# Softmax sums applied to outputs instead of probabilities, and modulation rows weighed on GpSimd, in a three-layer transformer kernel

## The reference, cut to what matters

```
shift, scale, gate = split(silu(c) @ ada_w + ada_b, 3)
h = rmsnorm(x, g) * (1 + scale) + shift
x = x + gate * mixer(h)
```

## Time and profile before

| | |
|---|---|
| median of 3 runs | 1159.05 us (1158.66 to 1159.08) |
| the profiled execution's own time | 1159.5 us |
| its span in the trace | 1157.7 us |
| busy in the span: PE, DVE, ACT, POOL | 1099.8, 734.3, 649.0, 419.3 us |
| layer 1's attention | about 106 to 398 us |
| layer 2's attention | about 565 to 752 us |

### The profile page before, as it was taken

The page is one execution under the profiler, slowest core; times in us unless marked ns, Lnnn a source line. Parts: engine busy times, 40 slices in busy tenths (PEclk is TensorE's granted clock), DMA queues, the critical chain, the costliest instruction groups (busy, mean ns, idle before and its releaser), DMA issues.

```text
span 1157.7 us, 20235 instructions
## 1 busy us (share of the span) xinstructions
PE 1099.8 (95%) x7430; PEld 900.7 (78%) x7430; DVE 734.3 (63%) x1590; ACT 649.0 (56%) x1355; POOL 419.3 (36%) x513
## 2 busy tenths in 40 slices
PE   5999999999998899999899999999999999999996
PEld 2678778877885689877688887898878777888785
DVE  7575766676568625363787787745767775527745
ACT  5604555555556526643677777846567753457733
POOL 2633012212120334675400002416654326456781
PEclk9999999999999999999999999999999999999998
DMA  9741424322114521130201101053212403213112
GB/s 373 253 163 46 176 107 162 133 108 101 46 29 173 204 81 37 40 109 35 57 14 34 65 10 47 1 166 87 73 46 78 151 19 128 91 56 121 44 37 73
DMA packets 34253, 109.33 MB, mean 94 GB/s; under 512 B 4516, under 2 KB 7076, under 8 KB 33772
## 3 DMA queue, kind: packets, MB, share of 16 engines
q1 hardware_dynamic: 34156, 108.05, 27.7%
HBM read 101.39 MB, written 2.11 MB: 89 GB/s over the span
## 4 chain that ended last, share of the span: by engine, by line
PE 75%; DVE 12%; ACT 5%; issue 3%; POOL 2%; DMA 2%; SPq 1%; DVEq 0%; POOLq 0%; ACTq 0%
PE PS L677 31%; PE PS L660 15%; PE PS L794 8%; PE PS L782 7%; PE PS L983 6%; PE PS L1051 3%; DMA AF<-wstream 2%; PE PS L712 2%; DVE AD L2372 1%; ACT AF L1272 1%; DVE AF L2069 1%; POOL AR L2553 1%; DVE AR L2273 1%; PE PS L884 1%; PE PS L693 1%
## 5 line engine op out<-in xcount | busy, mean ns | idle before, releaser
L2553 POOL TENSOR_TENSOR AR<-AF,AR 128x256 fp32r<-128x256 f32 x396 | 304.5, 802 | 585.2 <-ACT AR L1152 585.2
L677 PE MATMUL PS<-AR 128*128 128x512 f32 (+1 forms) x2208 | 450.5, 360 | 4.7 <-POOL AR L2553 1.4
L677 PEld LDWEIGHTS PS<-AR 128*128 128x128 f32 x2208 | 364.0, 189 | 72.6 <-issue 10.5
L660 PE MATMUL PS<-AR 128*128 128x256 f32 (+4 forms) x1284 | 244.9, 327 | 6.7 <-ACT AF L1272 1.7
L660 PEld LDWEIGHTS PS<-AR 128*128 128x128 f32 (+1 forms) x1284 | 179.8, 190 | 41.7 <-issue 20.6
L1281 ACT ACTIVATE AF<-PS 128x512 f32<-128x512 f32 (+3 forms) x192 | 124.6, 649 | 100.0 <-PE PS L782 96.0
L1272 ACT ACTIVATE AF<-PS,AF 128x512 f32<-128x512 f32 (+3 forms) x192 | 140.8, 733 | 27.2 <-DVE AF L2349 18.3
L782 PE MATMUL PS<-AF 128*128 128x128 f32 x864 | 127.4, 274 | 8.4 <-DVE AF L1990 5.9
L782 PEld LDWEIGHTS PS<-AF 128*128 128x128 f32 x864 | 100.1, 140 | 32.9 <-issue 15.5
L1152 ACT ACTIVATE AR<-AF 128x1024 fp32r<-128x1024 f32 x99 | 103.3, 1052 | 35.3 <-PE PS L983 27.9
L794 PE MATMUL PS<-AF 128*64 128x128 f32 x1728 | 115.3, 278 | 3.4 <-DVE AF L1997 2.5
(11 more groups left out here) (216 smaller groups left out, 1147.2 us busy)
## 6 DMA issues: line engine op xcount, KB each, us to landing
AF<-wstream SPq DMA_DIRECT2D x171, 512.0 KB, 5.0
AF<-x_in SPq DMA_DIRECT2D x2, 1024.0 KB, 8.5
AD<-rows SPq DMA_DIRECT2D x4, 512.0 KB, 5.9
out<-AF SPq DMA_DIRECT2D x16, 128.0 KB, 1.9
AF<-AF SPq DMA_DIRECT2D x28, 64.0 KB, 2.0
AF<-rpb_band SPq DMA_DIRECT2D x8, 224.0 KB, 5.2
BIAS<-rpb_band SPq DMA_DIRECT2D x8, 224.0 KB, 4.7
AF<-ctx_in SPq DMA_DIRECT2D x1, 1024.0 KB, 5.5
```

Source lines behind the costliest of these rows:

```text
L660: mm = pe.matmul(out, stationary, moving, start=i == 0, stop=i == len(products) - 1)
L677: mm = pe.matmul(out[:, 0:t1 - t0], a, b, start=k == 0 and i == 0, stop=k == nk - 1 and i == 2)
L2553: ins = pool.tensor_tensor(w[:, 1, at:at + 256], raw(c)[:, at:at + 256], w[:, 0, at:at + 256].bitcast(F32), ALU.subtract)
```

## The change

Three things are done.

First, for pairs 0 to 5 of layer 1 and 0 to 6 of layer 2 (`N_LATE`) the probabilities are no longer multiplied by the inverse sum. PE turns them as soon as the exponentials are done. ACT leaves the sums of a whole pair side by side. At the first step of the next pair DVE inverts them (`invert_sums`), SP stores the 128 x 12 or 128 x 8 numbers element by element into DRAM so that tokens lie in a row, waits until they are there, and loads each head's row broadcast over 64 partitions (`spread_sums`). One pair later DVE multiplies the gated output by these rows (`scale_output`).

Second, layer 3's modulation rows are no longer made of 48 matmuls in layer 1. GpSimd multiplies each raw piece in place by the condition's value for each of its rows, and adds the halves and the pieces (`mix_rows`), 24 pieces at the start of layer 2's attention; PE then sums over the partitions with 6 matmuls against ones (`mixed_rows`, filler of step 19), and transposes once, at step 23.

Third, the order of pieces changes: ada2 stands behind B.uq1 and ahead of B.o0, layer 2's modulation (ada1) spreads over layer 1's attention, with ada1.4 and ada1.5 in the last pair.

```diff
-ADA_GROUPS = {0: ((0,), (1,), (2,), (3,), (4, 5)), 1: (tuple(range(6)),), 2: ((0, 1, 2), (3, 4, 5))}
+ADA_GROUPS = {0: ((0,), (1,), (2,), (3,), (4, 5)), 1: (tuple(range(6)),), 2: (tuple(range(6)),)}
+N_LATE = {"A": 6, "B": 7, "C": 0}
...
 def between_a(p):
-    return (None, "ada1.0", "ada1.2", "ada1.4", "ada1.5.t", "ada2.1", None, None)[p]
-def late_a(p):
-    return (None, "ada1.1", "ada1.3", "ada1.5", "ada2.0", None, None, "ada2.2")[p]
+    return (None, "ada1.0", "ada1.1", "ada1.2", None, "ada1.3", None, None)[p]
...
-        return [["ada2.2.t"], ["ada2.3"], ["ada2.4"], ["ada2.5"], ["ada2.5.t"], late[0:1], late[1:3],
+        return [["ada1.4:0"], ["ada1.4:1"], ["ada1.5:0"], ["ada1.5:1"], ["ada1.5.t"], late[0:1], late[1:3],
...
 def fillers_b(p, step):
     if step == 3:
-        return []
+        return {5: ["mix2.sum"], 6: ["ada2.5.t"]}.get(p, [])
...
 def turn(n):
-    pe.wait_ge(p_ready, n + 1)
+    if late(n):
+        pe.wait_ge(exp_done, n + 1)
+    else:
+        pe.wait_ge(p_ready, whole_at[n] + 1)
...
+def mixed_rows():
+    out = acc_open("mix2.sum")
+    pe.wait_ge(mix_step, MIX_STEPS)
+    for b in range(6):
+        g = b % 4
+        mm = pe.matmul(out[32 * g:32 * g + 12, :], ONE_ROW[:, 10 - 2 * b:22 - 2 * b], MIXED[:, b],
+                       start=b < 4, stop=b >= 2)
...
+def scale_output(layer, p):
+    rows = SUM_ROWS[layer]
+    dve.wait_ge(sums_in, 32 * (late_at(layer, p) + 1))
+    ins = dve.tensor_tensor(OG[:, p, :], OG[:, p, :], rows[:, 0:S], ALU.mult)
...
+def mix_rows():
...
+    for b in range(6):
+        for q in range(4):
+            pool.wait_ge(*raw_loaded(c))
+            pool.tensor_tensor(w, w, by, ALU.mult).then_inc(mix_step, 1)
...
+            if summed:
+                add_to(*summed)
...
+            ins = pool.tensor_tensor(total, w[:, 0], w[:, 1], ALU.add)
...
-for first, after in ((2, "B.o1"), (4, "B.o2"), (6, "B.o5")):
+for p, after in ((2, "ada2.2.2"), (3, "ada2.3.2"), (4, "ada2.4.1"), (5, "ada2.5.1"), (6, "B.o0"), (7, "B.o4")):
     if name == after:
-        load_roped_queries(first)
-        load_roped_queries(first + 1)
+        load_roped_queries(p)
+        spread_sums("B", p - 2)
+        if p == N_PAIR - 1:
+            spread_sums("B", p - 1)
...
+def spread_sums(layer, p):
+    if p >= N_LATE[layer]:
+        return
+    n, i = per_pair[layer], late_at(layer, p)
+    sp.wait_ge(sums_ready, i + 1)
+    sp.dma_start(sums_dram[p % 2, 0:2 * n * P].rearrange("(i q) -> q i", q=P),
+                 SUMS_OF[layer][2][:, p % 2].rearrange("p h t -> p (h t)"), allow_slow_non_contiguous=True).then_inc(sums_stored, 16)
+    sp.wait_ge(sums_stored, 16 * (i + 1))
+    if i:
+        sp.wait_ge(scaled, i)
+    for h in range(2):
+        sp.dma_start(SUM_ROWS[layer][ROWS_OF[h], 0:n * P],
+                     sums_dram[p % 2:p % 2 + 1, h * n * P:(h + 1) * n * P].to_broadcast([64, n * P])).then_inc(sums_in, 16)
```

More of the change, by code:

```diff
@@ L68, in chunk_plan @@
         split(f"A.q{p}", f"A.g{p}")
[L69 to L72, removed]
+        name = between_a(p)
+        if name:
+            ada(int(name[3]), int(name[5]))
     split("A.o0")
-    for late in (3, 4, 5):
-        ada(2, late)
+    for late in (4, 5):
+        ada(1, late)
     split(*[f"A.o{j}" for j in range(1, KD)])
@@ L592, in is_c, with late, late_at, late_sums @@
             return n >= 2 * B_END
+        def late(n):
+            return units[n]["pair"] < N_LATE[units[n]["layer"]]
+        whole = [n for n in range(len(units)) if not late(n)]
+        whole_at = {n: i for i, n in enumerate(whole)}
+        def late_at(layer, p):
+            return p + (N_LATE["A"] if layer == "B" else 0)
+        def late_sums(n):
+            u = units[n]
+            t = n // 2 - start_of[u["layer"]] - per_pair[u["layer"]] * u["pair"]
+            sums, sinks = (SUMS_OF[u["layer"]][i][:, u["pair"] % 2] for i in range(2))
+            return sums[:, u["half"], t:t + 1], sinks[:, u["half"], t:t + 1]
         def score_bank(n):
@@ L721, in ada_columns @@
                 out = acc_open(name)
-                rows, i = tasks[f"ada{layer}.{b}"]
+                rows, i = tasks["mix2.sum" if layer == 2 else f"ada{layer}.{b}"]
                 pe.wait_ge(acc_read[rows], i)
@@ L1991, in normalise, with invert_sums, late_work @@
                                   ALU.mult).then_inc(p_ready, 1)
+            def invert_sums(layer, p):
+                dve.wait_ge(exp_done, pair_scored(layer, p))
+                sums, sinks, inverse = (SUMS_OF[layer][i][:, p % 2] for i in range(3))
+                if layer == "A":
+                    step(dve.tensor_tensor(sums, sums, sinks, ALU.add))
+                signal(dve.reciprocal(inverse, sums), sums_ready, late_at(layer, p) + 1)
+            def scale_output(layer, p):
+                rows = SUM_ROWS[layer]
+                dve.wait_ge(sums_in, 32 * (late_at(layer, p) + 1))
+                ins = dve.tensor_tensor(OG[:, p, :], OG[:, p, :], rows[:, 0:S], ALU.mult)
+                if layer == "A":
+                    ins = dve.tensor_tensor(OGC[:, p, :], OGC[:, p, :], rows[:, S:T], ALU.mult)
+                signal(ins, scaled, late_at(layer, p) + 1)
+            def late_work(layer, m):
+                n = per_pair[layer]
+                p, s = (m - start_of[layer]) // n, (m - start_of[layer]) % n
+                if s == 0 and 1 <= p <= N_LATE[layer]:
+                    invert_sums(layer, p - 1)
+                if s == 0 and 2 <= p <= N_LATE[layer] + 1:
+                    scale_output(layer, p - 2)
+                if s == n - 1 and p == N_LATE[layer] == N_PAIR - 1:
+                    scale_output(layer, p - 1)
             def gate_output(m):
@@ L2024, in attend @@
                         negmax(2 * m + 1)
+                    if m < m1 and not late(2 * m):
                         normalise(2 * m)
@@ L2027, in attend @@
                         gate_output(m - 2)
+                    if m < m1 and not late(2 * m):
+                        normalise(2 * m + 1)
                     if m < m1:
-                        normalise(2 * m + 1)
+                        late_work("A" if early else "B", m)
                     if later and m0 < m <= m1:
@@ L2764, in others @@
                     sp.dma_start(ROPE, rope[1]).then_inc(sp_rope, 16)
-                if name == "B.o0":
+                if name == "ada2.1.0":
                     sp.wait_ge(kr_split, 1)
@@ L3032 @@
     out = nc.dram_tensor("out", (P, KD, S), F32, kind="ExternalOutput").ap()
-    build(nc, rows_dram=rows_dram, out=out, **args)
+    sums_dram = nc.dram_tensor("sums", (2, 2 * T), F32, kind="Internal").ap()
+    build(nc, rows_dram=rows_dram, sums_dram=sums_dram, out=out, **args)
     result = run_bass_kernel_spmd(nc, [arrays], core_ids=[0]).results[0]["out"]
```

85 lines of the change are left out of this document (73 added, 12 removed).

## The result

The changed kernel takes 1178.43 us (median of 4 runs, 1177.94 to 1178.96), the kernel before 1159.07 in the same comparison: 1.0165 times as long, 95% interval 1.0148 to 1.0183, 19.3 us slower. The forecast was 1163.5, its range ended at 1176.

The account below looks back on a forecast made before the run. PE, busy for 95% of the span, was taken as the bound. -14.0 (layer 1) + 2.2 + 7.6 + 8.6 (layer 2) = +4.4 us gave 1163.5 us; own range 1161.5 to 1170, 8 in 10 1150 to 1176.

Parts of the forecast that it names:

- Layer 1: Layer 1's attention: removed matmuls and softmax work gain 14.0 us, 3.2 of it in the last pair; bounds 9 and 18.
- the 10 at which I feared for the splits: Layer 1: a store of sums over 10 us would use up its cover, costing the excess for each of 6 pairs.
- PE's work in layer 2: Layer 2: six matmuls on four column groups (1.8 us) and 4 transposes (0.4) lose 2.2 us.
- Waiting for GpSimd: Layer 2, step 19: PE waits 7.6 us for POOL, whose last pieces stand behind pair 3's store; bounds 3 and 14.
- Numbers of 4 bytes are nearer in bytes to nothing than to 3 KB: I take a third: Layer 2's store of 1024 numbers: a third of 9.6 us, 3.2, in all 5.0.
- the upper bound of 11.4: Layer 2's store of sums: 64 packets for each engine at 0.15 us, 9.6, in all 11.4 us.
- The lower bound: Step 19's wait for GpSimd: 3 us, with a store of 1.8 us and POOL's own pace deciding.
- Waiting for B.o4: Layer 2, step 28: B.o4's load behind pair 6's sums makes ACT 9.3 us late, PE loses 8.6; bounds 5.4 and 15.0.
- Rival 3: Dear stores: layer 2's waits +14 and +15 us, layer 1's cover nearly used, +17 in all, 1176; chance 0.12.
- Rival 1: Faster: store at most 1.8 us, POOL's product 2.0, only B.o4's wait (5.4) left, -10, 1149; chance 0.25 (waits under 10).
- Rival 4: GpSimd slowed 1.23 times by DVE through layer 2: PE's wait 28 us, time 1184; chance 0.04.
- Turning without normalisation gives nothing in steady pairs: Layer 2's steady pairs: late sums gain nothing, PE being full.

Follow-up runs that it names:

- late_only: The kernel before with the late inverse sums alone (N_LATE 6 and 7), modulation blocks of layer 3 still matmuls in layer 1: 1156.2 us.
- both_moved: The changed kernel with pair 6's sums stored behind B.o6's load and SP's earlier groups of queries and sums later between pieces: 1147.86 us, 0.9899 of the kernel before.
- no_late: The changed kernel with N_LATE of both layers at 0, so only the weighed modulation rows and new order of blocks remain: 1172.8 us.

## Why the prediction was wrong

The direction and the two waits in layer 2 came as described. Two steps failed: the terms of the waits were too small (16.2 us taken for both, 26.0 measured), the store above all (5.0 taken, 8.5 and 9.0 measured), and the sum had no term for PE's clock after a wait, 4.5 us.

**Layer 1, 14.0 predicted, 12.9 measured.** The gains of the pairs came out nearly as worked: 1.6, 1.6 and 1.8 us for the pairs with two blocks (1.7 taken), 0.8 (0.9), pair 6 1.1 (1.3); the pairs without a block gave more, 3.4 and 1.8 where 2.6 and 0.9 stood, since the whole wait for exponentials went. The last pair gave 0.5 where I took 3.2 (0.3 of the 12.9 lies outside the pairs). That term failed too: I costed blocks of PE in a pair in which DVE is busy for 31 of 38.5 us, and DVE got 1.1 us of scaling on top. The stores took 10.9 to 12.2 us, over the 10 at which I feared for the splits, and nothing came of it.

**PE's work in layer 2, 2.2.** Right: `late_only` to `both_moved`, 353.4 to 355.7.

**Waiting for GpSimd, 7.6 predicted, 10.2 measured.** The mechanism is the one described, and its terms can be read one by one: store 8.95 (5.0 taken), issues 1.2 (1.1), landing 5.8 (4.2), POOL's rest from the piece on 13.2 (16.2). 7.6 + 3.9 + 0.1 + 1.6 - 3.0 = 10.2. The mis-sized term is the store. "Numbers of 4 bytes are nearer in bytes to nothing than to 3 KB: I take a third" was the wrong scale, and so was the scale it started from, the time of a packet on an engine (0.15 us for 3 KB): the store's packets took some 7 ns each, and the wait went on for 6.8 us after the last of them. That the upper bound of 11.4 lay near the dearest stores (11.0) is luck. The lower bound was slipped as well: with a store of 1.8 the piece would land at 666.0, after POOL's 664.5, and the same sum gives a wait of 4.4, not 3. POOL also starved at earlier stores (11.2 us at pair 2's), which I had not looked for; it did not show, because the last piece was later still.

**Waiting for B.o4, 8.6 predicted, 15.8 measured.** Store 8.5 (+3.5), landing 6.0 (+1.8), and the sums exist 2.0 later relative to ACT than I read, because DVE first normalises the two units of pair 7, which is not late, and inverts after them. 8.6 + 3.5 + 1.8 + 2.0 = 15.9.

**Missing from the sum: the clock.** 2.6 us after the first wait (3.59 - 1.89 + 2.20 - 1.32) and 1.9 after the second (1.51 - 0.85 + 2.77 - 1.53). I costed a wait of PE at its length.

**Together.** 2.2 + 10.2 + 2.6 + 15.8 + 1.9 - 1.4 (what late sums give in layer 2, by late_only) = 31.3 of the 31.5. With -12.9 and the 0.6 of the rest that is the 19.2. Rival 3 (dear stores, 14 and 15 us) was the nearest; its 1176 had the first wait 3.8 too long and lacked the clock's 4.5, so that it came this near partly by luck. Rival 1 had GpSimd's product right (2.0, measured 1.93) and nothing else. Rival 4, GpSimd slowed by DVE, did not happen (products of 1.93 us); its mirror image, DVE slowed by GpSimd, would have, had the sums not become late. "Turning without normalisation gives nothing in steady pairs" was true for the kernel before (1.4 us for the whole layer) and is worth 15 us as soon as GpSimd works: the two parts of the change belong together, which my part-by-part sum could not see.

## What to carry to other kernels

Count the pieces of a DMA, not its bytes alone, and price it by how long its waiter waits, not by how long the engines are busy. If an engine waits for it, count everything that stands behind that wait in the engine's list; here moving two such waits by a few places turned 1.6% slower into 1.0% faster. Give a long wait of PE something for its clock: here 2.6 us for one of 10.2 and 1.9 for one of 15.8. When work moves to GpSimd, look at what DVE does in SBUF at the same time, single-input products too, and look at the parts of a change in pairs.

## What the runs showed of the hardware

- 1024 numbers of 4 bytes into DRAM: 8.5 to 11.0 us until the wait ends in the changed kernel (8.0 to 11.6 in all runs with such stores); 1536: 10.9 to 12.2; the bytes of the 1024 in 128 runs: 1.4 alone, 3.4 to 4.4 behind pieces of weights. At step 28 the engines' packets end 6.8 us before the wait does.
- DVE's product of 128 x 768 fp32 with a number per partition, SBUF to SBUF: 0.64 to 0.66 us, beside GpSimd's products and additions 1.48 on average, 2.36 at most. GpSimd's own rose from 1.93 to 2.05 (products) and from 1.27 to 1.38 (additions) on average.
- `no_late`, in a pair without a block, has a granted clock of 0.66 in the 5 us behind a wait of PE of 1.67 us, and the kernel before, in a pair of the same shape behind a wait of the same 1.67 us, 1.00. What decides between them is open. `no_late` first:

```profile
241.00:246.00 5.00, 3.17 (x31) 2.38 (x29) 4.79 (x12) 2.77 (x10) 0.00 (x0) 1.00 0.00 2
246.00:251.00 5.00, 4.75 (x23) 3.86 (x22) 4.28 (x14) 3.25 (x9) 2.83 (x4) 0.66 0.10 14
```
```profile
317.00:322.00 5.00, 3.33 (x31) 2.59 (x29) 4.77 (x12) 2.27 (x8) 0.00 (x0) 1.00 0.00 0
322.00:327.00 5.00, 4.59 (x29) 3.64 (x29) 4.54 (x15) 3.67 (x11) 2.87 (x4) 1.00 0.01 3
```
